# Last FFN1 block by thirds of tokens, the next norm carried into the same program block, and the first third's low parts on GpSimd

## What is computed

```python
x = x + 0.5 * gate1 * swiglu(h, w_ffn1_in, w_ffn1_out)
h = modulate(rmsnorm(x, g_mix), shift2, scale2)     # rmsnorm: x * rsqrt(mean(x*x) + EPS) * g
z = h @ w_in                                        # columns: u, v, q, k, vm, o, 8 gates, g_a, g_b
v = layernorm(gelu(z[..., 1024:2048]), ln_g, ln_b)
gif = z[..., 6144:6152] + b_gates                   # input and forget gates of 4 heads
```

## Time and profile before

| | us |
|---|---|
| median of 3 runs | 2886.97 (2883.53 to 2889.72) |
| the profiled execution | 2888.01 |
| its span, first to last instruction | 2886.2 |
| PE busy in the span | 2803.4 (97%) |
| DVE, ACT, POOL busy | 1424.4, 844.4, 109.9 |

### The profile page before, as it was taken

One profiled execution on the slowest core, in us unless ns is written; L12 is line 12 of the kernel. 1 busy time (PEld: TensorE's weight loads), 2 busy tenths in 40 slices (PEclk: granted clock), 3 DMA queues, 4 the chain that ended last, 5 costly groups with the idle time before them and its releaser, 6 DMA issues. The chain is left out here.

```text
span 2886.2 us, 44186 instructions
## 1 busy us (share of the span) xinstructions
PE 2803.4 (97%) x17385; PEld 2717.1 (94%) x17385; DVE 1424.4 (49%) x3004; ACT 844.4 (29%) x1370; POOL 109.9 (4%) x176
## 2 busy tenths in 40 slices
PE   7899999999999898999999999999899999999998
PEld 5899999999999798999999999999899999999998
DVE  5644555555444736346446435634764444444445
ACT  4422222222212522342343244244521111111113
POOL 0000000000002100000000000000300000000002
PEclk9999999999999899999999999999999999999999
DMA  7232232322210205122121222212111111111111
GB/s 239 88 103 73 87 102 87 102 87 87 73 44 16 60 16 151 43 71 82 50 66 56 68 64 69 75 51 66 52 44 44 44 44 44 44 44 44 44 44 63
DMA packets 171140, 196.84 MB, mean 68 GB/s; under 512 B 9197, under 2 KB 160009, under 8 KB 170966
## 3 DMA queue, kind: packets, MB, share of 16 engines
q1 hardware_dynamic: 170578, 194.98, 21.2%
q10 hardware_dynamic: 342, 0.15, 0.0%
q0 software_dynamic: 96, 0.00, 0.0%
HBM read 174.65 MB, written 18.89 MB: 67 GB/s over the span
## 5 line engine op out<-in xcount | busy, mean ns | idle before, releaser
L680 DVE SCALAR_TENSOR_TENSOR xT<-ps,gate_p,xT 128x384 f32<-128x384 f32 (+1 forms) x624 | 347.0, 570 | 112.7 <-PE ps L1089 99.9
L1240 PE MATMUL ps<-hhi,mw_hi 128*128 128x384 f32 (+1 forms) x1152 | 384.0, 333 | 9.3 <-DVE mw_lo L2051 7.6
L974 DVE TENSOR_TENSOR hf<-st,ps 128x384 f32<-128x384 f32 x132 | 70.2, 532 | 644.9 <-PE ps L1110 644.0
L1241 PE MATMUL ps<-hlo,mw_hi 128*128 128x384 f32 (+1 forms) x1152 | 379.2, 329 | 0.0
L1242 PE MATMUL ps<-hhi,mw_lo 128*128 128x384 f32 (+1 forms) x1152 | 379.0, 329 | 0.0
L1108 PE MATMUL ps<-hhi,wa_hi 128*128 128x384 f32 (+1 forms) x1040 | 344.9, 332 | 6.7 <-DVE wa_lo L964 5.2
L1087 PE MATMUL ps<-g_hi,wo_hi 128*128 128x384 f32 (+1 forms) x1056 | 347.0, 329 | 0.0
L1089 PE MATMUL ps<-g_hi,wo_lo 128*128 128x384 f32 (+1 forms) x1056 | 346.3, 328 | 0.0
L1088 PE MATMUL ps<-g_lo,wo_hi 128*128 128x384 f32 (+1 forms) x1056 | 345.6, 327 | 0.0
L1109 PE MATMUL ps<-hlo,wa_hi 128*128 128x384 f32 (+1 forms) x1040 | 342.9, 330 | 0.0
L1110 PE MATMUL ps<-hhi,wa_lo 128*128 128x384 f32 (+1 forms) x1040 | 342.6, 329 | 0.0
(11 more groups left out here) (344 smaller groups left out, 5051.6 us busy)
## 6 DMA issues: line engine op xcount, KB each, us to landing
mw_raw<-in_w_in SPq DMA_DIRECT2D x32, 1024.0 KB, 6.0
ada_raw<-in_w_ada SPq DMA_DIRECT2D x28, 1024.0 KB, 5.1
wa_raw<-in_w_ffn_in SPq DMA_DIRECT2D x22, 1024.0 KB, 5.1
wb_raw<-in_w_ffn_in SPq DMA_DIRECT2D x22, 1024.0 KB, 5.2
wo_raw<-in_w_ffn_out SPq DMA_DIRECT2D x22, 1024.0 KB, 5.0
ada_first<-in_w_ada SPq DMA_DIRECT2D x8, 1024.0 KB, 12.7
ada_raw<-in_w_ada_final SPq DMA_DIRECT2D x8, 1024.0 KB, 5.3
cs<-in_state_mlstm_C SPq DMA_DIRECT2D x32, 256.0 KB, 2.8
```

The lines of the kernel that those rows point to most:

```text
L680: ins = dve.scalar_tensor_tensor(out=xT[:, m, t0:t0 + wp], in0=ps[:, bank, 0:wp], scalar=gate_p[:, m:m + 1], in1=xT[:, m, t0:t0 + wp], op0 ...
L974: dve.tensor_tensor(M["hf"][:, t0:t0 + w], M["st"][:, t0:t0 + w], ps[:, up_bank("b", b, i, n), 0:w], ALU.mult).then_inc(C["hidden"].sem, 1)
L1240: pe.matmul(out, wh, xh, start=(j == 0), stop=False)
L1241: pe.matmul(out, wh, xl, start=False, stop=False)
```

## The change

In the last block of the first FFN the output units go by thirds (`N_ORDER`: all slices of the first third, then of the second, then of the third). The norm that follows, and the whole of `gates_and_v`, is moved into that FFN's program block: there is no barrier between. What used to be `Norm.means`, `roots` and reciprocals of whole rows is done by token: PE sums `rr` into one column per 128 tokens (`sums`, three small matmuls per third), ACT takes the root of 128 x 3 numbers, DVE inverts them and writes three diagonal matrices, and PE spreads these over the partitions into a PSUM bank (`spread`); `turn` reads its factor there. The first third is normed between the units of the third third: DVE turns slice `k` at unit 15 + `k`, ACT makes the high part and the shifted sum, and POOL the low part, in its queue behind the adds of squares. Gate weights and the first quarter of v's weights are loaded and split during the output units. `rest` on DVE does the second and third thirds.

```diff
+            def sums(self, pe, n):
+                pe.wait_ge(*self.sq.added((KT - 1) * (n + 1)))
+                if n == 1:
+                    pe.wait_ge(*self.rms_done(1))
+                if n == 2:
+                    pe.wait_ge(*self.t_done(KT))
+                for t, a in self.tiles(n):
+                    ins = pe.matmul(ps[:, self.SUMS[n], t:t + 1], rr[:, a:a + P], mean[:, 0:1], start=True, stop=True)
+                ins.then_inc(self.mean_done.sem, 1)
...
+            def inverse(self, dve, n):
+                dve.wait_ge(*self.rms_done(n + 1))
+                dve.reciprocal(inv_t[:, 3 * n:3 * n + 3], rms_t[:, 3 * n:3 * n + 3]).then_inc(*dve_steps.one())
+                if n:
+                    dve.wait_ge(*self.spread_done(n))
+                dve.wait_ge(*dve_steps.now())
+                for t, a in self.tiles(n):
+                    ins = dve.tensor_scalar(diag[:, t % 3, :], ident[:, :], inv_t[:, t:t + 1], float(D), ALU.mult, ALU.mult)
...
+            def spread(self, pe, n):
+                pe.wait_ge(*self.inverse_done(n + 1))
...
+            def high_and_sum(self, act, k):
...
+                act.activation(hhi[:, k, t0:t0 + w], t, ACT.Identity, bias=bias)
+                act.activation(t, t, ACT.Identity, bias=bias).then_inc(self.hi_done.sem, 1)
+
+            def low_of_sum(self, pool, k):
+                t0, w = UNITS[0]
+                pool.wait_ge(*self.hi_done(k + 1))
+                pool.tensor_tensor(hlo[:, k, t0:t0 + w], self.ring[:, k % RINGS, 0:w], hhi[:, k, t0:t0 + w].bitcast(F32),
+                                   ALU.subtract).then_inc(self.lo_done.sem, 1)
+
+            def out_scalar(self, act, u):
+                if u == 12:
+                    self.root(act, 0)
+                if 15 <= u < 15 + KT:
+                    self.high_and_sum(act, u - 15)
+                if u == 22:
+                    self.root(act, 1)
+
+            def out_vector(self, dve, u):
...
+                if u == 13:
+                    self.inverse(dve, 0)
+                if u == 15:
+                    dve.wait_ge(*self.spread_done(1))
+                if 15 <= u < 15 + KT:
+                    self.turn(dve, u - 15)
+
+            def out_gpsimd(self, pool, u):
+                if 16 <= u < 16 + KT:
+                    self.low_of_sum(pool, u - 16)
+
+            def out_tensor(self, pe, u):
+                if u == 12:
+                    self.sums(pe, 0)
+                if u == 15:
+                    self.spread(pe, 0)
+                if u == 21:
+                    self.sums(pe, 1)
+
+            def rest(self, dve):
+                self.inverse(dve, 1)
+                for n in (1, 2):
+                    dve.wait_ge(*self.spread_done(n + 1))
+                    for k in range(KT):
+                        self.turn(dve, n * KT + k)
+                        if n == 1 and k == 5:
+                            self.inverse(dve, 2)
+                        if k >= 2:
+                            self.low(dve, n * KT + k - 2)
...
+        N_ORDER = [(m, n) for n in range(3) for m in range(KT)]
...
                             if p == 0 and t % 3 == 0:
                                 gate(t // 3)
+                                if t == 0:
+                                    norm.spread(pe, 1)
+                            if (p, t) == (0, 2):
+                                norm.sums(pe, 2)
+                            if (p, t) == (0, 5):
+                                norm.spread(pe, 2)
```

More of the change, by code:

```diff
@@ L364, in samples @@
[L364 to L373, removed]
+                                  ALU.add).then_inc(self.t_done.sem, 1)
@@ L558, in vector @@
                     self.keep(dve, 1)
[L559 removed]
+                    dve.wait_ge(*norm.rms_done(3))
                     def pair(i):
@@ L711, in ffn @@
             C = ffn_counts
-            sq = Squares(final.order if final else OUT_ORDER)
+            LAST_ORDER = final.order if final else N_ORDER if to else OUT_ORDER
+            sq = Squares(LAST_ORDER)
+            if final:
+                final.sq = sq
+            if to:
+                to.norm.sq = sq
             ADA_BLOCKS = (ALL_T // 2 - FIRST_ADA) // 4 if lead else 0
@@ L1042, in body @@
                         up(b, ada_too)
-                        for u, (m, n) in enumerate(final.order if final and last else OUT_ORDER):
+                        for u, (m, n) in enumerate(LAST_ORDER if last else OUT_ORDER):
                             if final and last and u == 19:
@@ L1050, in body @@
                             add_out(dve, own, m, n, out_bank(u, last), M["tmp"][:, m % 4, :, :], C["x_added"])
+                            if to and last:
+                                to.out_vector(dve, u)
+                                to.norm.out_vector(dve, u)
                             if final and last and u == 16:
@@ L1176, in body @@
                                 ada_turn(pe, group(b, 3))
+                            if to and last:
+                                to.norm.out_tensor(pe, u)
                             if final and last:
@@ L1357, in _, with scalar @@
                     pool.tensor_tensor(S["rstd"][:, :], S["rstd"][:, :], M["half"][:, :], ALU.pow).then_inc(rstd_done.sem, 1)
[L1359 to L1373 removed]
+                def scalar(self, act):
+                    for j in range(KT, 2 * KT):
                         norm.high(act, j)
+                        if j == KT + 3:
+                            norm.root(act, 2)
                     for p in range(4):
@@ L1421, in link @@
                         dve.wait_ge(*own.now())
-                    norm.factors(dve)
-                    norm.unit(dve, 0, between=lambda: low(1, gate_lo, gate_raw, gate_hi))
-                    split(0)
-                    norm.unit(dve, 1)
-                    norm.unit(dve, 2)
+                    norm.rest(dve)
                     norm.samples(dve)
@@ L1510, in _, with tensor @@
                     dve.wait_ge(*own.now())
-                @block.tensor
-                def _(pe):
-                    norm.means(pe)
+                def tensor(self, pe, x_added):
                     wh, wl = gate_hi, gate_lo
@@ L2557, in layer @@
         head_w_in = [cnt("h_w_in0"), cnt("h_w_in1")]
-        S = gates_and_v(M, after, ar.at, v, Norm(V_MIX, 24, 32, gate=40, factor=1.0), m_d, a_d)
+        S, gates = gates_and_v(M, after, ar.at, v, NextNorm(V_MIX, 24, 32, gate=40, factor=1.0, at=top), m_d, a_d)
+        ffn(I["w_ffn1_in"][0], I["w_ffn1_out"][0], first_norm, lead=lead, to=gates)
         stored = spatial(M, S, after + NTT * D * 4, v, mixed_d)
```

236 lines of the change are left out of this document (154 added, 82 removed).

## The result

The changed kernel takes 2889.44 us (median of 20 runs, 2885.19 to 2894.73), the kernel before, run beside it, 2884.24 (20 runs, 2879.70 to 2889.72). The ratio is 1.0016, with a 95% interval of 1.0009 to 1.0022: 5.2 us slower by the medians, clear of zero, and less than the 0.2% that the prediction calls a difference. The forecast was a kernel 2.3 us slower.

A forecast was written before the change was run, and what follows sets the result against it. PE was taken to bound the kernel, with only idle and half-clock stretches to win (18.7 us). Gate(2) 1.2 us earlier, plus clock losses of 2.0 and 1.5, gave +2.3: median 2886.97 to 2889.3 us, range 2883.5 to 2896.

The forecast's parts named there:

- two clock losses: PE at half clock after idling: 2.0 us lost behind the wait ahead of gate(2), 1.5 us around gate(0)'s end.
- the idle before gate(2): Sign of being right: PE idle of about 7 us ahead of gate(2), behind the samples.
- the steps of POOL: Sign of being right: POOL unbroken from about 938 to 952 in steps of 1.9 us, feeding gate(0) slice by slice.
- a stall of PE at spread(0): Sign of being wrong: PE waits at spread(0), where no wait, or up to 1.6 us, was expected.
- Part 1: Output units up to the first turn: root done at 932.6, diagonals 0.22 us each, first turn done at 935.1.
- the rival with the lock between DVE and POOL: DVE and POOL hold each other up during the first third's norm: POOL steps over about 2.1 us, 2894.7 us; chance 0.16.
- Part 2: First third's norm between the last units: POOL paces at 1.89 us a step, gate(0) ends at 952.5, 9.1 us gained.
- Part 3: From gate(0) to gate(2): DVE's 9.9 us behind spread(2) leave PE idle 7.2 us; gate(2) at 983.5, 1.2 us gained.
- the last third is not late: Rival: gate(2) follows tile 5 at once, at 976.3, 8.4 us early; 2880.1 us; chance 0.06.
- Part 4: Half clock after PE idles: 2.0 us lost (1.2 to 2.9) from the wait before gate(2), 1.5 (0 to 2.9) from POOL's pacing.
- The rival in which the clock holds in gate(0): PE's clock holds, or falls and recovers before the tiles, while POOL paces gate(0); 2886.5 to 2887.8 us; chance 0.23.
- POOL no help: Rival: POOL's low parts take over 2 us, gate(0) ends at 961, all 9 us are gone; 2898 us; chance 0.02.

The follow-up runs named there:

- The experiment with the table early: Against the changed kernel, ACT loads the root's table at unit 9 by an extra root and the diagonals stay on DVE; 2889.29 us in one run.
- the filled wait: Against the changed kernel, 36 matmuls that nothing reads fill PE's wait ahead of gate(2); 2886.58 us, ratio 1.0010 to the kernel before.
- six low parts on POOL: Changed kernel with spread(2) early, diagonals on ACT, table early, and the first third's last two low parts on DVE; 2873.85 us, 0.9963 of before.

## Why the prediction was right or wrong

**The direction and the mechanism held.** The forecast was that 9 us won ahead of tile 0 would be lost in a new wait ahead of gate(2), with two clock losses on top. The distance to tile 0 did fall, the new wait is there, and both clock losses are. The forecast of the change was +2.3; by tile 6 it is +5.23. That the absolute time agrees so closely, 2889.3 against 2889.44, is luck: the runs of before shown ahead had a median of 2886.97 and the ones beside after 2884.24. The difference is what is to be judged, and it came out 2.9 us larger than forecast. Of the signs that the prediction names, the idle before gate(2), the steps of POOL and the half clock behind came. Gate(2) itself came at 71.56, just behind the 66 to 71 (982 to 987) that it gives; and a stall of PE at spread(0), which it lists among the signs of being wrong, came too.

**Part 1 is the term that was mis-sized: spread(0).** The prediction took no wait there ("or up to 1.6 us"); PE waits 2.44. The lines of ACT and DVE show two terms that were too small: the root ends 1.3 us later than predicted, and the diagonals take 1.1 us longer.

```profile
928.93 1.58 ACT L200 ACTIVATE norm_ring<-xT 128x384 f32<-128x384 f32 x3 [1.41 <-DVE xT L792]
930.52 1.28 ACT L404 ACT_TABLE_LOAD   x1
931.82 0.26 ACT L404 ACTIVATE norm_rms<-ps,eps_col 128x3 f32<-128x3 f32 x1
...
927.14 1.23 DVE L1429 TENSOR_TENSOR mw_lo<-mw_raw,mw_hi 128x1024 fp32r<-128x1024 f32 x1 [1.02 <-ACT mw_hi L1425]
928.28 2.19 DVE L792 SCALAR_TENSOR_TENSOR xT<-ps,gate_p,xT 128x384 f32<-128x384 f32 x4
932.11 0.17 DVE L409 RECIPROCAL norm_inv<-norm_rms 128x3 f32<-128x3 f32 x1 [1.65 <-ACT norm_rms L404]
932.32 1.74 DVE L414 TENSOR_SCALAR norm_diag<-ident,norm_inv 128x128 f32<-128x128 f32 x3
```

- *The root is late.* It ends at 932.08, 17.88 after S; the prediction had 16.56 (932.6). DVE's split of the weights waits 1.02 us for ACT's half and takes 1.23, and the adds of four units stand behind it and come in a row at 928.28. So ACT squares three in a row, from 928.93, and can load its table only at 930.52; the load itself took the 1.28 us that the prediction gave it. The prediction counted the added splits as lying in slack, from the busy shares of the earlier trace rows. As a share DVE had that slack; but splits and units are in one queue, and the unit that the root needs stood behind a split. That is read from the rows: no run moved the splits. The experiment with the table early leaves them where they are and takes the load out of the chain instead; the 1.13 us that it wins show that PE's wait hangs on when the root is done.
- *The diagonals take 0.58 us each,* against the 0.22 assumed, 1.74 for three. POOL is adding squares beside them, four in a row from 929.53 to 933.98. Where POOL has nothing to do, at inverse(2), the same three take 0.68, and in inverse(1), beside POOL's back-to-back work, 2.37:

```profile
949.92 2.37 DVE L414 TENSOR_SCALAR norm_diag<-ident,norm_inv 128x128 f32<-128x128 f32 x3
...
962.69 0.68 DVE L414 TENSOR_SCALAR norm_diag<-ident,norm_inv 128x128 f32<-128x128 f32 x3
```

The price of 0.22 was read from a free DVE and holds there. Of the rival with the lock between DVE and POOL, this part came true: it had put 1.0 more on the diagonals; they took 1.1 more. The Trainium skill, SBUF — State Buffer, section "Who interferes with whom", counts tensor_scalar among the operations that can contend with GpSimd, in a two-port mode; the rows agree, 0.68 to 1.74 and 2.37 for three, and the product of three numbers at 829 ns.

**Part 2, POOL's pace, was sized well.** The groups of 912 to 954 us, which answer to the earlier trace rows:

```profile
L210 POOL TENSOR_TENSOR rr<-rr,norm_ring 128x384 f32<-128x384 f32 x14 | 16.0, 1141 | 149.3 <-ACT norm_ring L200 148.0
...
L440 POOL TENSOR_TENSOR hlo<-turned,hhi 128x384 fp32r<-128x384 f32 x8 | 8.0, 1003 | 0.0
...
L210 POOL TENSOR_TENSOR rr<-rr,norm_ring 128x320 f32<-128x320 f32 x7 | 6.1, 872 | 1.2 <-ACT norm_ring L200 1.2
L802 DVE TENSOR_TENSOR xT<-xT,ffn_tmp 128x64 f32<-128x64 f32 x8 | 5.3, 667 | 0.3
...
L342 DVE SCALAR_TENSOR_TENSOR turned<-xT,gp,ps 128x384 f32<-128x384 f32 x8 | 4.8, 604 | 0.0
```

The low part takes 1003 ns (predicted 1010), the narrow add 872 (880). POOL sets the pace, without a break from 939.62 to 952.20, in steps of 1.79 (945.03 to 946.81 in the rows below) where 1.89 was predicted. The tenth is overlap: the low part starts at 945.86, before the add ahead of it is done at 945.90, which the prediction counted for DVE and ACT and not for POOL. The rival's stretched chain, steps of over 2.1, did not come. The turn, whose factor lies in PSUM, takes 604 ns, no more than L680 with one PSUM operand in before; the sample adds take 667 instead of 569. By the same section of the Trainium skill the first doesn't contend and the second does; the trace agrees. Seven of the eight sample adds were stretched, to 0.68 us and more; but POOL's own instructions kept their lengths, and DVE had the time in a step that POOL sets, so the stretching cost the chain nothing.

```profile
945.03 0.87 POOL L210 TENSOR_TENSOR rr<-rr,norm_ring 128x320 f32<-128x320 f32 x1
945.86 1.00 POOL L440 TENSOR_TENSOR hlo<-turned,hhi 128x384 fp32r<-128x384 f32 x1
946.81 0.87 POOL L210 TENSOR_TENSOR rr<-rr,norm_ring 128x320 f32<-128x320 f32 x1
...
951.21 0.99 POOL L440 TENSOR_TENSOR hlo<-turned,hhi 128x384 fp32r<-128x384 f32 x1
```

The last low part ends 38.0 after S, predicted 35.9. Spread(0) is 2.46 late and POOL's unbroken run begins 0.30 later still, less 0.65 for seven quicker steps. The last slice behind it took 1.01 at half clock (952.26 to 953.27) instead of 0.52. So gate(0) ends 2.6 late, and gate(2), at 71.56 instead of 69.0, is late by the same 2.6: from there to gate(2) every term held.

**Part 3, the new wait, was right.** Predicted 7.2 us of idle, measured 6.89. DVE's first turn behind spread(2) starts at 975.84, and from there to DVE's last instruction (984.97 + 0.69 = 985.66) it is 9.82 us, predicted 9.9:

```profile
975.84 1.26 DVE L342 SCALAR_TENSOR_TENSOR turned<-xT,gp,ps 128x256 f32<-128x256 f32 x3 [8.78 <-PE ps L424]
...
984.97 0.69 DVE L374 TENSOR_TENSOR hlo<-norm_samples,hhi 128x512 fp32r<-128x512 f32 x1 [0.69 <-ACT hhi L304]
```

The bracket shows DVE idle for 8.78 us until spread(2), with everything but the factor at hand. Writing spread(2) two tiles earlier takes the idle away altogether, as the run with that edit shows. The rival "the last third is not late" failed in after for the reason that the prediction gave, PE's written order, and that order is all that stood against it.

**Part 4, the clock, was right within its bounds.** Gate(2) takes 2.30 us longer than in before, predicted 2.0 (1.2 to 2.9), and the filled wait shows that it is the clock. From spread(1) to the first turn behind spread(2) it took 22.6 us, predicted 20.9 + 1.5. The rival in which the clock holds in gate(0) fell: 0.51 from 950 to 957.

**POOL no help** is half true in another way than that rival had it: POOL's low parts are no slower than was thought, but on DVE they end earlier (36.4 against 38.0 after S, and tile 0 at 39.21 against 40.21). Giving them to POOL brings nothing.

Summed up: +2.6 for spread(0) and what hangs on it and +0.3 for the clock, on the +2.3 forecast, give the 5.2 measured. Behind tile 6 the two traces run alike up to a wait of 3.4 us that both have, 41.05 us later; the half clock behind that wait was longer by 1.2 us in after (the q transposes stand 95.58 behind tile 6, 94.39 in before). That is one trace of each, and the cause of the 1.2 stays open; by FFN2's first matmul it is made up, which stands 1087.2 us behind tile 6 in after and 1087.9 in before.

## What to carry to other kernels

A wait that is removed at the head of a chain is worth only what the order written further down lets through: look for the step in each engine's program that a later stage needs, and move it up in the same edit; here that step, spread(2), was worth 10 us by tile 6 (0.3% of the time by the two ratios), and the whole restructuring ahead of it gained nothing without it. A small instruction that a whole engine waits for is priced by what stands ahead of it in its queue and what runs beside it, not by its free duration or the engine's busy share. Where a wait can't be moved, count its length and then the half clock behind it.

## What the runs showed of the hardware

- Short DVE operations on SBUF were stretched beside a busy POOL: a tensor_scalar of 128x3 took 829 ns, where a reciprocal of as many took 0.17 us; three 128x128 in 1.74, 2.03 and 2.37 us against 0.68; a 128x64 add 667 ns against 226, and 331 where POOL had no low parts to make.
- It went both ways: POOL's wide adds took 1141 ns on the mean in after, where DVE's weight splits and diagonals lie beside them, against 1013 in before and 1015 with the new order alone; and a split of 512 columns took DVE 1.29 us, where L374 took 0.69 over as many columns with POOL at rest:

```profile
L1429 DVE TENSOR_TENSOR gate_lo<-gate_raw,gate_hi 128x512 fp32r<-128x512 f32 x1 | 1.3, 1290 | 0.1
```

- PE, fed one slice in 1.8 us, fell to the lower level as it did behind the wait of 6.89 us (0.51 from 950 to 957 and 0.55 in gate(2), in after; 0.67 from 944 to 954 with six low parts on POOL). Matmuls that nothing reads kept it at 1.00 at both places.
